# A two-block transformer kernel on one core: gains of two norms folded into weight splits, latent norms from raw products, and a new order at the conv end and in the heads

## What is computed

```python
def rms_norm(x, g):
    y = xf * lax.rsqrt(jnp.mean(xf * xf, axis=-1, keepdims=True) + RMS_EPS)
    return (y * g.astype(jnp.float32)).astype(x.dtype)
...
def conformer_conv(h, ...):
    u = h @ w_pw1 + b_pw1
    a, gate = jnp.split(u, 2, axis=-1)
    u = a * jax.nn.sigmoid(gate)
    u = depthwise convolution of width 31 over tokens + b_dw
    u = jax.nn.silu(layer_norm(u, ln_g, ln_b))
    return u @ w_pw2 + b_pw2
...
def mla_shared_kv(h, kv_in_g, w_dkv, kv_norm_g, w_kr, w_uk, w_uv, cos, sin):
    hn = rms_norm(h, kv_in_g)
    c_kv = rms_norm(hn @ w_dkv, kv_norm_g)
    k_rope = apply_rope(hn @ w_kr, cos, sin)
    k_nope = (c_kv @ w_uk).reshape(b, s, N_HEADS, QK_NOPE_DIM)
    v = (c_kv @ w_uv).reshape(b, s, N_HEADS, V_HEAD_DIM)
...
def mla_attention(hn, w_dq, q_norm_g, w_uq, ...):   # hn = rms_norm(h, mix_pre_g[1])
    q = (rms_norm(hn @ w_dq, q_norm_g) @ w_uq).reshape(b, s, N_HEADS, QK_HEAD_DIM)
```

## Time and profile before

| | us |
|---|---|
| median of three executions | 1166.9 |
| lowest, highest | 1166.52, 1168.44 |
| profiled execution | 1168.28 |
| its span, first to last instruction | 1166.4 |
| PE busy | 1143.9 |
| DVE busy | 828.7 |
| ACT busy | 657.9 |
| POOL busy | 131.6 |

### The profile page before, as it was taken

One profiled execution on the slowest core, in us unless ns is written; L12 is line 12 of the kernel. 1 busy time (PEld: TensorE's weight loads), 2 busy tenths in 40 slices (PEclk: granted clock), 3 DMA queues, 4 the chain that ended last, 5 costly groups with the idle time before them and its releaser, 6 DMA issues.

```text
span 1166.4 us, 26682 instructions
## 1 busy us (share of the span) xinstructions
PE 1143.9 (98%) x10651; PEld 974.7 (84%) x10651; DVE 828.7 (71%) x1320; ACT 657.9 (56%) x1019; POOL 131.6 (11%) x168
## 2 busy tenths in 40 slices
PE   9999999999999999999999999999999999999998
PEld 7778888888778888888877688888887778888887
DVE  6786777655786886655569759777666666987664
ACT  7664675433667476433475657564456656765432
POOL 0000200000203200000243220000124531000010
PEclk9999999999999999999999999999999999999999
DMA  8661375555362465555453337654575343755451
GB/s 338 259 206 53 103 245 208 178 187 211 113 249 96 136 240 190 206 182 185 152 203 109 110 109 254 211 175 149 181 256 181 110 165 107 262 192 190 149 178 56
DMA packets 31468, 206.59 MB, mean 177 GB/s; under 512 B 3488, under 2 KB 3872, under 8 KB 10144
## 3 DMA queue, kind: packets, MB, share of 16 engines
q1 hardware_dynamic: 31104, 205.00, 51.3%
q10 hardware_dynamic: 288, 0.52, 0.1%
HBM read 204.46 MB, written 1.05 MB: 176 GB/s over the span
## 4 chain that ended last, share of the span: by engine, by line
PE 89%; DVE 7%; ACT 2%; issue 1%; POOL 0%; DVEq 0%
PE ps L617 20%; PE ps L618 20%; PE ps L619 20%; PE ps L970 2%; DVE w_lo L2233 2%; PE ps L741 1%; PE ps L1397 1%; PE ps L880 1%; PE ps L648 1%; PE ps L1399 1%; PE ps L1398 1%; PE ps L726 1%; PE ps L882 1%; PE ps L881 1%; PE ps L643 1%
## 5 line engine op out<-in xcount | busy, mean ns | idle before, releaser
L1480 ACT ACTIVATE w_hi<-staged 128x2048 f16<-128x2048 f32 (+2 forms) x195 | 344.8, 1784 | 237.8 <-PE ps L619 229.2
L617 PE MATMUL ps<-f_hi,w_hi 128*128 128x256 f16 x1596 | 435.0, 273 | 0.2 <-issue 0.2
L618 PE MATMUL ps<-f_lo,w_hi 128*128 128x256 f16 x1596 | 435.0, 273 | 0.0
L619 PE MATMUL ps<-f_hi,w_lo 128*128 128x256 f16 x1596 | 435.0, 273 | 0.0
L2233 DVE SCALAR_TENSOR_TENSOR w_lo<-staged,w_hi 128x2048 f16<-128x2048 f32 (+2 forms) x195 | 415.0, 2142 | 24.2 <-ACT w_hi L1480 24.0
L617 PE MATMUL ps<-x_hi,w_hi 128*128 128x256 f16 x696 | 189.8, 273 | 0.6 <-DVE tmp L2586 0.6
L618 PE MATMUL ps<-x_lo,w_hi 128*128 128x256 f16 x696 | 189.7, 273 | 0.0
L619 PE MATMUL ps<-x_hi,w_lo 128*128 128x256 f16 x696 | 189.7, 273 | 0.0
L618 PEld LDWEIGHTS ps<-f_lo,w_hi 128*128 128x128 f16 x1596 | 156.2, 98 | 19.3
L617 PEld LDWEIGHTS ps<-f_hi,w_hi 128*128 128x128 f16 x1596 | 156.2, 98 | 18.6 <-issue 0.4
L619 PEld LDWEIGHTS ps<-f_hi,w_lo 128*128 128x128 f16 x1596 | 156.2, 98 | 18.0
(11 more groups left out here) (375 smaller groups left out, 1790.9 us busy)
## 6 DMA issues: line engine op xcount, KB each, us to landing
staged<-weights SPq DMA_DIRECT2D x165, 1024.0 KB, 5.2
staged<-weights SPq DMA_DIRECT2D x32, 704.0 KB, 4.3
xn<-bands SPq DMA_DIRECT2D x3, 512.0 KB, 9.9
m<-bands SPq DMA_DIRECT2D x3, 512.0 KB, 8.0
cst<-constants SPq DMA_DIRECT2D x1, 1027.0 KB, 7.9
h<-x_turned SPq DMA_DIRECT2D x2, 512.0 KB, 4.6
staged<-weights SPq DMA_DIRECT2D x2, 512.0 KB, 6.9
qT<-bands SPq DMA_DIRECT2D x2, 512.0 KB, 11.5
```

The lines of the kernel that those rows point to most:

```text
L617: pe.matmul(out, wh, xh[:, c, :], start=(c == 0), stop=False)
L618: pe.matmul(out, wh, xl[:, c, :], start=False, stop=False)
L619: last = pe.matmul(out, wl, xh[:, c, :], start=False, stop=(c == kc - 1))
L1480: act.activation(w_hi[:, s, o:o + n], staged[:, s, o:o + n], ACT.Copy, scale=SW).then_inc(hi_split, 1)
```

## The change

Four edits in one.

**Input norms.** The gains of kv and of dq go into the weights: the splits of these two units multiply each 384-column block (the three outputs of one input chunk, laid out anew on the host) by a column of `vec` in place of the constant SW. That is `with_gain` on ACT and on DVE, 8 instructions for each unit in place of 2. The input is then split once, into f_hi and f_lo, and x_hi and x_lo of this norm are gone (8 instructions on ACT, 8 on DVE). All three kv outputs are made in the loop, and dq from the same input, both by chunk and then output.

**Latent norms.** Squares are taken by ACT from the raw products, the input norm's row factor cancels, and its eps terms are added as one more float32 matmul for each of the two sums (`eps_terms`). The steps on DVE are put in another order, the reciprocal of the input norm's root moves to the end, where only the rotary key needs it, and swap(0) moves from between the ukv products to behind the second uq product.

**Conv end.** Half of convolve(6) goes behind the last `copy_rows`, half of convolve(7) behind L1001; the table load for Sqrt goes behind `convolved(6)`; on DVE `shift(7)` goes ahead of a weight split and a reciprocal ahead of the centring; 10 of the 45 fill matmuls go.

**Heads.** Weight splits and the mask go behind steps that PE waits for, on ACT and DVE, in the even heads and ahead of the last moba pair; on PE some products of the output projection and `swap_query(3)` go elsewhere.

```diff
-            def convolve(j):
...
+            def convolve(j, first=0, end=TAP_STEPS):
...
                 gate_or_value(2 * j + 1)
-                convolve(j - 1)
+                if j < DC - 1:
+                    convolve(j - 1)
+            convolve(DC - 2, 0, TAP_STEPS // 2)
             copy_rows(DC - 1)
+            convolve(DC - 2, TAP_STEPS // 2)
             sum_bands(range(0, 4))
-            sum_bands(range(4, 6))
-            sum_bands(range(6, 7)).then_inc(group_summed, 1)
-            convolve(DC - 1)
+            sum_bands(range(4, 7)).then_inc(group_summed, 1)
+            convolve(DC - 1, 0, TAP_STEPS // 2)
             pe.wait_ge(group_taken, 2)
...
+            convolve(DC - 1, TAP_STEPS // 2)
             fill(5, 2)
...
-            fill(10, 2)
+            fill(3, 2)
             pe.wait_ge(ln_step, 3)
             rows_of(8, 7).then_inc(ln_rows, 1)
-            fill(24, 4)
+            fill(21, 4)
...
-            together("kv", 2, f_hi, f_lo, "mix_pre_1")
+            def with_gain(name, first, c):
+
+                u = FIRST[name]
+                if c % (DC // 2) == 0:
+                    arrived(2 * u + c // (DC // 2))
+                o = gained_columns(c).start
+                for j in range(3):
+                    wh, wl = weights(u % 2, o + P * j, P)
+                    pe.matmul(ps[:, first + j, 0:T], wh, f_hi[:, c, :], start=(c == 0), stop=False)
+                    pe.matmul(ps[:, first + j, 0:T], wl, f_hi[:, c, :], start=False, stop=False)
+                if name == "kv":
+                    pe.wait_ge(x_lo_ready, SPLIT_AT["mix_pre_1"] + c + 1)
+                for j in range(3):
+                    wh, wl = weights(u % 2, o + P * j, P)
+                    last = pe.matmul(ps[:, first + j, 0:T], wh, f_lo[:, c, :], start=False, stop=(c == DC - 1))
...
+            def latent_sums(name):
+
+                pe.wait_ge(rooted, NORM_AT[name])
+                pe.wait_ge(eps_terms, len(LATENT))
+                pe.matmul(STAT, k("ones"), tmp[:, LATENT.index(name), :], start=True, stop=False)
...
+            for c in range(DC):
+                if c:
+                    add_square("mix_pre_1", c - 1)
+                pe.wait_ge(x_hi_ready, SPLIT_AT["mix_pre_1"] + c + 1)
+                with_gain("kv", 0, c)
             add_square("mix_pre_1", DC - 1)
...
+            for c in range(DC):
+                with_gain("dq", 4, c)
+                if c == 2:
+                    latent_sums("kv_norm")
...
                 if j == 2:
-                    sums("q_norm")
-                if j == 3:
-
-                    pe.wait_ge(drained["dq"], 3)
-                    swap(0)
+                    latent_sums("q_norm")
...
+                if j == 1:
+
+                    pe.wait_ge(key_scaled, 1)
+                    swap(0)
...
-            act.activation(by_token[:, 0:1], by_token[:, 11:12], ACT.Sqrt)
             shift(DC - 1)
             convolved(DC - 2)
+            act.activation(by_token[:, 0:1], by_token[:, 11:12], ACT.Sqrt)
...
             root("kv_norm")
-            square_latent(0)
-            square_latent(1)
+            split(2 * FIRST["kv"] + 4)
             his("kv_norm", f_hi[:, 8:10])
-            square_latent(2)
-            act.wait_ge(product["dq"], 3)
-            split(2 * u0 + 4)
+            split(2 * FIRST["kv"] + 5)
+            latent_squares("q_norm", (4, 5, 6), "dq")
+            split(2 * FIRST["dq"] + 4)
...
             exp_pair("even", 2)
-            even_split(11, 11)
             fox_rows(14, 3, 1)
             high_pair("even", 1)
+            even_split(11, 11)
...
-                for g in LOW_SPLITS[j][-1:]:
-                    split(g)
+                if j < DC - 1:
+                    for g in LOW_SPLITS[j][-1:]:
+                        split(g)
             shift(DC - 1)
+            split(LOW_SPLITS[DC - 1][-1])
...
+            dve.wait_ge(group_taken, 3)
+            dve.reciprocal(by_token[:, 8:10], by_token[:, 6:8]).then_inc(ln_step, 1)
             dve.wait_ge(ln_rows, 1)
             centre(0)
-            dve.wait_ge(group_taken, 3)
-            dve.reciprocal(by_token[:, 8:10], by_token[:, 6:8]).then_inc(ln_step, 1)
...
+            with_gain("dq", range(DC))
+            dve.wait_ge(rooted, NORM_AT["mix_pre_1"] + 1)
+            for e, name in enumerate(LATENT):
+                n = NORM_CHUNKS[name]
+                dve.tensor_scalar(tmp[:, e, :], STAT, n * RMS_EPS / D, n * RMS_EPS ** 2, ALU.mult, ALU.add).then_inc(eps_terms, 1)
+            invert("kv_norm")
+            scale("kv_norm", 0, (f_hi[:, 8:10], f_lo[:, 8:10]))
+            split(2 * FIRST["kv"] + 4)
+            split(2 * FIRST["kv"] + 5)
+            invert("q_norm")
+            scale("q_norm", 4, (f_hi[:, 10:13], f_lo[:, 10:13]))
+            split(2 * FIRST["dq"] + 4)
             invert("mix_pre_1")
...
+            dve.tensor_tensor(kT[:, 8, :], kT[:, 8, :], LATE_SCALE, ALU.mult).then_inc(key_scaled, 1)
             rope(0)
...
-            chain(dve.tensor_scalar(sel[:], idx[:, TOPK // 8 % 2, :], TAKEN / 2, MASKED, ALU.is_gt, ALU.mult))
-            chain(dve.tensor_tensor(sel[:], sel[:], k("causal"), ALU.add))
-
-            even_split(11)
+
             reduce_pair("even", 3)
             add_rope_keys(0)
+            even_split(11)
             invert_pair("even", 3)
             low_pair("even", 2)
             rope_query(0)
+            chain(dve.tensor_scalar(sel[:], idx[:, TOPK // 8 % 2, :], TAKEN / 2, MASKED, ALU.is_gt, ALU.mult))
+            chain(dve.tensor_tensor(sel[:], sel[:], k("causal"), ALU.add))
...
-            for g in ODD_SPLITS[last_pair - 1][1:]:
-                split(2 * u0 + g)
+            split(2 * u0 + 13)
             invert_pair("moba", last_pair - 1)
             low_pair("moba", last_pair - 2)
             rope_pair(last_pair)
+            split(2 * u0 + 14)
```

More of the change, by code:

```diff
@@ L1066, in _ @@
             pe.wait_ge(late_loaded, 48)
-            together("kv", 2, f_hi, f_lo, "mix_pre_1")
-            add_square("mix_pre_1", DC - 1)
-            linear("kv", 3, f_hi, f_lo, done=2)
-            u = FIRST["dq"]
-            for j in range(3):
-                if j != 1:
-                    arrived(2 * u + j // 2)
-                features(ps[:, 4 + j, 0:T], u % 2, j * D, DC, x_hi, x_lo,
-                         None if j else lambda c: pe.wait_ge(q_in_lo, c + 1)).then_inc(product["dq"], 1)
-                if j == 0:
-                    sums("kv_norm")
+            def with_gain(name, first, c):
[12 more added lines that the diff above has]
+                    last = pe.matmul(ps[:, first + j, 0:T], wh, f_lo[:, c, :], start=False, stop=(c == DC - 1))
+                    if c == DC - 1:
+                        last.then_inc(product[name], 1)
@@ new lines, in latent_sums @@
+            def latent_sums(name):
+                pe.wait_ge(rooted, NORM_AT[name])
+                pe.wait_ge(eps_terms, len(LATENT))
+                pe.matmul(STAT, k("ones"), tmp[:, LATENT.index(name), :], start=True, stop=False)
+                for c in range(NORM_CHUNKS[name]):
+                    pe.wait_ge(squared, SQUARE_AT[name] + c + 1)
+                    last = pe.matmul(STAT, k("ones"), sq[:, c, :], start=False, stop=(c == NORM_CHUNKS[name] - 1))
+                last.then_inc(summed, 1)
@@ L1486, in split, with with_gain @@
                     hi(g, g // 2 % 2, 16 * (g // 4 + 1), n, o)
+            def with_gain(name, chunks):
+                s = FIRST[name] % 2
+                for c in chunks:
+                    g = 2 * FIRST[name] + c // (DC // 2)
+                    at = gained_columns(c)
+                    act.wait_ge(landed[s][g % 2], 16 * (g // 4 + 1))
+                    ins = act.activation(w_hi[:, s, at], staged[:, s, at], ACT.Copy, scale=v(WEIGHT_GAINS[name], c))
+                    if c % (DC // 2) == DC // 2 - 1:
+                        ins.then_inc(hi_split, 1)
             def quarter(g, q):
@@ L1778, in mlp @@
                     unit(i, 1)
-                unit(units // 2 - 1, 0)
+                if layer == 0:
+                    act.wait_ge(gains_scaled, 2)
+                    act.wait_ge(product[two], units - 1)
+                    with_gain("kv", range(DC))
+                else:
+                    unit(units // 2 - 1, 0)
                 last_square(product[two], DC, ps[:, 1, 0:T], INVF)
@@ L2604, in mlp, with unit @@
                 chain(dve.memset(stat[:, 3, :], 0.0))
-                def unit(i, s, splits=True):
+                def unit(i, s, splits=True, squares=False):
                     dve.wait_ge(product[two], i * 2 + (s + 1))
-                    if not splits:
+                    if not splits and not squares:
                         dve.wait_ge(last_squared, BY_TOKEN.index(f"ffn_post_{layer}") + 1)
@@ L2623, in mlp @@
                     unit(i, 1)
-                unit(last, 0)
+                unit(last, 0, layer == 1, True)
+                if layer == 0:
```

(8 more changed lines are left out.)

140 lines of the change are left out of this document (73 added, 67 removed).

## The result

| | before | changed |
|---|---|---|
| median of 6 executions each, us | 1167.6 | 1161.2 |
| lowest, highest | 1164.91, 1169.88 | 1159.57, 1162.27 |
| profiled execution (span) | 1168.28 (1166.4) | 1161.21 (1159.3) |
| PE busy | 1143.9 | 1140.2 |

The ratio is 0.9948, interval 0.9933 to 0.9962: 6.1 us faster, between 4.4 and 7.8. The forecast was 6.3, and 1160.6.

What follows compares the result with a forecast made beforehand. PE's own work plus a few waits and two slow-clock stretches bound the kernel; conv end -3.0, latent +2.8, heads -5.4, moba -0.7 sum to -6.3 us, so 1160.6 us, range for 8 in 10 1157.5 to 1164.

Steps and rivals of the forecast that it cites:

- Wait ahead of ukv: Latent attention: PE waits 1.4 us for the ukv split where it waited 0.15, +1.25 us, no slow stretch.
- Wait at swap(3): Latent attention, uq products: PE newly waits 2.35 us for rope(1), with a slow stretch behind, +1.7 us.
- slow stretch: PE's clock at 1.2 in place of 2.4 GHz behind a wait of about 2.0 us, costing 1.7 us each.
- Stage +2.8: Latent attention as a whole costs 2.8 us, between -0.4 and +4.5.
- rival (d): Kv loop: f_lo blocked for a whole POOL add, period 1.65 in place of 1.41, +0.7 us, 1161.3; chance 0.07.
- The gain of the loop (-3.4): Kv loop: without x_lo PE becomes slower than DVE and its waits vanish, 6 x 0.57 = -3.4 us.
- the price of the eps terms (+0.87): Latent attention: two float32 matmuls for eps cost PE 0.87 us.
- Heads and moba: Even heads -5.4 us from waits and a slow stretch that go; ahead of the last moba pair -0.7 us.
- rival (b): Even heads: a new wait (mask or rope query) replaces the old, about 1 us plus 1.7 slow stretch, 1163.3; chance 0.12.
- the wait of 1.99 that ends with ACT's square of chunk 6: Conv end, ahead of the sums: ACT's shorter chain cuts PE's wait to 0.9 us, -1.1 us.
- rival (c): Conv end: PE waits for something other than ACT's chain, only -0.4 us stays, 1163.2; chance 0.08.
- The clock terms: Slow stretches: -1.7 us at the conv end, -1.7 in the even heads, +1.7 behind swap(3).

Runs made afterwards that it cites:

- latent_mended: Changed kernel with another latent-stage order: first ukv and uq splits moved into idle time, three splits ahead of rope(0); 1157.76 us, ratio 0.9927 to the kernel before.
- before_count_84: The kernel before with only its PE program made 84 instructions longer by small warm-up matmuls at the start; 1162.65 us, ratio 0.9971.
- act_later: Changed kernel with two more useless squares on ACT between the last copies' high parts and convolve(6)'s take-out; 1163.29 us, ratio 0.9956 to the kernel before.
- fill6_swap3: Changed kernel with 6 fill matmuls (0.65 us) put into PE's wait at swap(3); 1160.18 us, ratio 0.9948 to the kernel before.
- heads_alone: The kernel before with only the edits of the even heads and of the last moba pair; 1161.37 us, ratio 0.9962.
- the shifted kernels: latent_mended with PE's program 84 or 168 instructions longer by small warm-up matmuls at the start; 1155.52 and 1155.17 us, ratios 0.9892 and 0.9890.

## Why the prediction was right, and where not

**Latent attention, right by its steps.** Loop period 1.41 forecast, 1.41 measured. Wait ahead of ukv 1.4, 1.37. Wait at swap(3) 2.35, 2.27. A slow stretch behind the second and none behind the first. Stage +2.8, measured +3.0, and with latent_mended both causes are shown. The rival (d), by which f_lo would be blocked behind POOL's add for its whole length, is out: the period would have been 1.65, and DVE by itself went at 0.87 a chunk beside POOL's adds, with f_lo written at 0.56 for 0.47 elsewhere. The gain of the loop (-3.4) and the price of the eps terms (+0.87) were not measured apart.

**Heads and moba, right.** -5.4 and -0.7 forecast, -5.4 and -0.66 measured. The new wait of rival (b) is there, on the rope query, but at 0.42 and not about 1, and without a slow stretch; the spare of 0.5 us that I had counted does not exist.

**Conv end, half wrong.** The failing step is "the wait of 1.99 that ends with ACT's square of chunk 6", from which I took -1.1. ACT's chain did become shorter as forecast, its end 1.25 us behind PE's last start in place of 2.44, but the sums start 2.08 behind it in place of 2.38: PE waited for something else. Start and end agreed in the trace of before to 0.06 us, by chance: the block of instructions came at the same moment. The sentence behind it, that the row shows chunks waiting whose squares had long been there, was the sign, and I made it a rival (c) with 0.08 where it deserved much more. Of -3.0 came -2.1: the clock -1.7 as forecast, the wait -0.2 in place of -1.1, the rest (L1001 and the layer norm's chain) -0.2 as said. Rival (c) is right in its cause and wrong in its price, since the slow stretch went all the same.

**The clock terms, right in the trace, too large for the median.** I took the two slow stretches of the profiled execution as there in every one. The 53 executions of the kernel before that ran beside the experiments, by the granted clock of the whole span:

| clock | executions | median, us |
|---|---|---|
| 0.994 or 0.995 | 15 | 1169.0 |
| 0.996 or 0.997 | 20 | 1166.7 |
| 0.998 and above | 18 | 1164.8 |

A stretch of 3.4 us at half clock is 0.0015 of the span, so these are about two, one and none, 2 us apart. The split is rough: every trace ends at half clock for another 0.9 to 4.0 us, which the reading takes in, and a trace that reads 0.998 can have one stretch (before_count_84, act_later) or none (fill6_swap3). The profiled execution had two, the median one by its reading has one. That fits the 1.4 us between them, which I carried over to the changed kernel as if it were a constant. The changed kernel had 0.999 or 1.000 in four of six executions. The prediction's two cases of a lowered clock left out this end of the trace, and its "largest 2.0 us" the wait of 2.5 at the start; neither entered the sum.

**No term, and -2.1 in the profiles.** Ahead of convolve(6) the two programs are the same. In the seven traces taken later with the length unchanged there, convolve(6) starts between 79.5 and 81.3, by pauses at 476 and 603 that come or don't, and by how early the clock rises after the start (the last warm-up matmul at half speed starts at 8.25 us in the trace of before and at 6.12 in that of the changed kernel). The profile of the changed kernel was a lucky one at 79.0; together with the clock terms, too large by about the same, this is why the total came out so near. The total was better than its reasons.

## What to carry to other kernels

Before a wait is put down to the engine named in its row, ask whether the first waiting instruction needs that result at all; if not, move the named engine (here by 0.87 us) and see whether the wait follows. Where one engine runs hundreds of short instructions, count them: a pause that keeps its place in the count and not in the program may be cured, as it was here, by a few instructions more at a point where they cost nothing. And where an edit moves work off an engine in one phase, write down what that engine does in the next, in order: the loss of 3.0 us in the latent stage could be read from a few rows, and was mended by moving a few calls.

## What the runs showed of the hardware

PE's stream of instructions can be what binds. In convolve and the copies PE starts a matmul every 0.02 to 0.03 us. There it paused 0.5 to 2.4 us (start to start) at block boundaries: longest, 2.0 to 2.4, behind a block of 3.1 to 3.3 us (records 1237 to 1364), shorter behind blocks of 4.6 to 6.2 us. The pace alone does not decide, since in the changed kernel and in heads_alone the blocks ahead of 476 and 603 took as long and no pause came. Behind the conv end, where a matmul takes 0.109 us or more, the waits above half a microsecond are the same in the shifted kernels as in latent_mended: none of them hangs on the count. The Trainium skill, page "Runtime: NRT & Kernel Launch", section "Instruction fetch mechanics", says that an engine's instructions come in blocks of 16 KiB, 256 instructions, the next fetched while the current one runs, and that this is mostly hidden. The size agrees with the counts above; hidden it was not at these places, and the measurement decides.

A wait's length alone does not say whether the clock falls behind it. In the heads, a wait of 1.97 (L1196) had the slow stretch in all four traces that kept it, at half clock from 0 to 0.7 us behind its end; other executions of the kernel before read 0.999 (12 of 53), which leaves hardly any room for it. In the kernel before with 84 instructions more:

```profile
643.00:647.00 4.00, 3.82 (x15) 2.66 (x16) 1.75 (x5) 0.97 (x5) 2.08 (x4) 0.57 0.53 219
```

At swap(3), 2.27 had it in all three traces, 1.52 did not in its one trace. At the conv end, waits of 1.7 to 2.0 in the new order had none in seven traces, and in the old order 1.9 to 2.0 had it in two of three, in one of these only behind the second pause, after convolve(7). What of PE's work ahead of the wait makes the difference stays open; no run was made for it.
